# A third fixed expert whose gate-up is loaded as the routing begins, and routing tables moved out of its buffer

## The chip, the cores and the metric

The kernel runs on one core of a Trainium2 chip. The time is device microseconds of one execution, the median of three runs. The profile is of one more execution of the same program. TensorE (PE) multiplies and turns matrices, VectorE (DVE) and ScalarE (ACT) do element work, GpSimd (POOL) element work and indirect DMAs (gathers and scatters by row index), SP issues plain DMAs. All DMAs, whoever issues them, run on the core's 16 DMA engines.

## The reference, cut to what matters

The program is two layers of a decoder, 1024 tokens of 1024 channels, float32. Each layer is a mixer (attention with a state-space scan in layer 0, a convolution module in layer 1) and then a mixture of 32 experts, each token going to two. Only the mixture is touched:

```
g_sel = argmax(xt @ w_group + b_group)                 # 1 of 4 groups
top_v, top_i = top_k((xt @ w_expert)[group g_sel], 2)  # 2 of its 8 experts
gu = xb @ w_gate_up[e]                                 # 1024 x 1024 per expert
y  = (silu(gu[:, :512]) * gu[:, 512:]) @ w_down[e]     # 512 x 1024 per expert
out[token] += gate * y
```

An expert's weights are 4 MB (gate-up) and 2 MB (down); all 32 are read in each layer.

## The kernel before, in words

The function `moe(k, layer)` does one mixture. It has two stages.

Routing. TensorE turns the tokens and forms the logits, VectorE chooses groups and experts, ranks the tokens of each expert and builds index tables: `hidx` (which rows each expert gathers), `yidx` (where each result goes), `order` (the experts sorted by their token count) and the overflow lists. Meanwhile ScalarE writes the normalised rows `h` of all eight 128-token tiles, two at a time, into a staging buffer for four tiles and stores each pair to HBM (`h_rows`, 1 MB a store). The copy of tile 4 waits for the first store, that of tile 6 for the second (`h_stored`).

Experts. Three buffers for gate-up (`wgu[0..2]`, the first of them lies in `early_gu`) and three for down (`wd[0..2]`, the first in `early_wd`) are used in turn: place q of the sequence uses buffer q % 3. The first `FIXED` places hold experts 0, 1, ... in that order; the others are sorted by count and placed by `place_of`, so that places with more and with fewer tiles alternate. Each place has a fixed number of 32-token blocks (`CAP`), 84 blocks in all. For each place GpSimd gathers the rows (`gather`, three buffers), TensorE turns them (`turn_tokens`), and for each block does gate-up and, one block later, down; ScalarE and VectorE form the hidden rows, ScalarE copies the result out, GpSimd scatters it. SP issues the loads in a list in program order: the load of place q waits on `gu_done` (down: `d_done`) for place q-3.

Where the routing tables lie: in the third pair of buffers, `wgu[2]` (the staging rows `h` and a part of the tables) and `wd[2]` (the rest). So the loads into the third pair wait until the tables are done with: gate-up on `y_index`, down on `over_ready`. The lines on SP:

```
load_down(sp, 1, 1)
for n in range(2):
    sp.wait_ge(h_stored[n], 16 * NT // 4)
load_gate_up(sp, 1, 1)
sp.wait_ge(order_ready, 1)
for q in range(FIXED, NE):
    e = sp.value_load(order[0:1, q:q + 1], ...)
    if q == 2: sp.wait_ge(y_index, 1)
    else:      sp.wait_ge(gu_done, last_of[q - 3] + 1)
    load_gate_up(sp, e, q % 3)
    ...
```

The gate-up and down of expert 0 are loaded before the function begins. The first gathers wait for all stores (`h_stored`) and for `h_index`. "Gate-up 5" below means the gate-up load of place 5, counted from 0.

Of the kernel before, what the change touches and what calls it, by code (L numbers as in the profile page):

```python
# [21 lines left out]
P = 128  # L22
D = 1024
T = 1024
NT = T // P
KD = D // P
# [13 lines left out]
NG, EG = 4, 8  # L40
NE = NG * EG
FF = 512
KF = FF // P
# [3 lines left out]
LN_EPS = 1e-5  # L47
MAX_OVER = NE
TB = 32
FIXED, FULL, LARGE = 2, 2, 14  # L50


XB, YB = 3, 6
TURNS, LAST_FULL = 12, 18
SQUARED_EARLY = 6
LOGITS_EARLY = (0, 3)

# [906 lines left out]
def moe(k, layer):  # L964
# [13 lines left out]
    with ExitStack() as ctx:  # L978
# [2 lines left out]
        wgu12, wd12 = sb("wgu", [P, 2, KD, 2 * FF]), sb("wd", [P, 2, KF, D])  # L981
        wgu = [first_gate_up(k), wgu12[:, 0, :, :], wgu12[:, 1, :, :]]
        wd = [first_down(k), wd12[:, 0, :, :], wd12[:, 1, :, :]]
        third = [wgu[2].rearrange("p k n -> p (k n)"), wd[2].rearrange("p k n -> p (k n)")]
        behind = [k.early_gu[:, KD * 2 * FF + NE * n:KD * 2 * FF + NE * (n + 1)] for n in range(7)]
        used = [0, 0]

        def early(shape, b=0):
            n = math.prod(shape[1:])
            flat = third[b][:, used[b]:used[b] + n]  # L990
            used[b] += n
            assert used[b] <= (KD * 2 * FF, KF * D)[b]
            if len(shape) == 2:
                return flat
            names = "abc"[:len(shape) - 1]
            return flat.rearrange(f"p ({' '.join(names)}) -> p {' '.join(names)}", **dict(zip(names, shape[1:])))

        n_over = sb("n_over", [P, 1], I32)
        over_expert = sb("over_expert", [P, MAX_OVER], I32)
# [2 lines left out]
        yidx = sb("yidx", [P, P // TB, NE], I32)  # L1002

        ss, rstd = k.m_ss, k.m_rstd
        h = early([P, 4, D])
        xT = sb("xT", [P, 2, KD, P])
        L = k.logits
        strict = early([P, P], 1)
        desc = behind[0]
        eid = behind[1]  # L1010
        pos_row = early([P, P], 1)
        quarter = sb("quarter", [P, 1])
        iota_i = sb("iota_i", [P, P], I32)
        quarter_i = sb("quarter_i", [P, 1], I32)
# [1 line left out]
        slot_ids = sb("slot_ids", [P, 2, NT], I32)  # L1016
        slot_next = sb("slot_next", [P, 2 * NT])
        pad = sb("pad", [P, MAX_OVER], I32)
        scan_mask = early([P, NE, NT + 1])
        gm, gw, wm = sb("gm", [P, NT]), sb("gw", [P, NT]), sb("wm", [P, NT])  # L1020
        ge, go = sb("ge", [P, NT, NG]), sb("go", [P, NT, NG])
        E, W = early([P, NT, NE], 1), early([P, NT, NE], 1)
        M = early([P, 2, NT, NE], 1)
        M_flat = M[:, :, :, :].rearrange("p j i e -> p (j i) e")
        Msel = early([P, 2, NT, NE], 1)
        Msel_flat = Msel[:, :, :, :].rearrange("p j i e -> p (j i) e")
        both = early([P, NE, NT + 1], 1)
        top = [sb("top1_", [P, NT]), sb("top2_", [P, NT])]
        ex, den = sb("ex", [P, NT]), sb("m_den", [P, NT])
        pre = early([P, NE, NT + 1], 1)  # L1030
        rank = early([P, NE, NT], 1)
        rank_sel = early([P, 2 * NT])
        in_group, met = early([P, NT, EG]), early([P, NT, EG])
        key = early([P, NE], 1)
        cmp = early([P, NE, NE], 1)
        V_rank = cmp[:, 0:2 * NT, :]
        nth = early([P, NSORT], 1)
        up_to = early([P, NSORT], 1)
        place = early([P, NE], 1)
        V = early([P, 2 * NT, NE])  # L1040
        R = early([P, 2 * NT, P])
        tabT = early([P, P], 1)
        tabT_rows = early([P, P // TB, P])
        fold = behind[2]
        fold_sorted, place_col = early([P, NE]), early([P, 1])
        empty, wrap, hf = early([P, NE]), early([P, NE]), early([P, NE])
        empty_y, yf = early([P, P // TB, NE]), early([P, P // TB, NE])
        order_f = early([P, NE], 1)
        cap_e, excess = early([P, NE], 1), early([P, NE], 1)
        extra, incl, shift, oe = behind[3], behind[4], behind[5], sb("oe", [P, MAX_OVER])  # L1050
        one_row = behind[6]
        pos, posf = sb("pos", [P, 2 * NT], I32), sb("posf", [P, 2 * NT])

        xg = sb("xg", [P, XB, D])
        sg = sb("sg", [P, 2, P])
        hh = sb("hh", [P, 2, P])
        hhT = sb("hhT", [P, 2, P])
        y = sb("my", [P, YB, D // 4])
        over_y = R[:, 0:NT, :].rearrange("p n t -> p (n t)")
        over_hh = R[:, NT:NT + KF, :]  # L1060
        over_sg = R[:, NT + KF:2 * NT, :].rearrange("p n t -> p (n t)")
        over_slot = sb("over_slot", [P, 1], I32)
        over_h = sb("over_h", [P, 1])
        over_ih = sb("over_ih", [P, 1], I32)
# [10 lines left out]
        dve_link, pool_link = sem("m_dve_link"), sem("m_pool_link")  # L1075
        gu_loaded = [k.dma_sems[layer]["gu_loaded0"]] + [sem(f"gu_loaded{p}_") for p in range(1, 3)]
        wd_loaded = [k.dma_sems[layer]["wd_loaded0"]] + [sem(f"wd_loaded{p}_") for p in range(1, 3)]
        zeroed = sem("zeroed")
        gathered = [k.dma_sems[layer][f"gathered{n}"] for n in range(XB)]
        stored = [k.dma_sems[layer][f"stored{n}"] for n in range(YB)]  # L1080
        turned, xT_ready, gu_done, silu_ready, hh_ready = sem("e_turned"), sem("xT_ready"), sem("gu_done"), sem("silu_ready"), sem("hh_ready")
# [30 lines left out]
        @block.sync  # L1112
        def _(sp):
            sp.wait_ge(consts, 1)
            sp.dma_start(k.token_slot.rearrange("(p n) a -> p (n a)", p=P), pad[:]).then_inc(padded, 16)
            load_down(sp, 1, 1)
            for n in range(2):
                sp.wait_ge(h_stored[n], 16 * NT // 4)
            load_gate_up(sp, 1, 1)
            sp.wait_ge(order_ready, 1)  # L1120
            for q in range(FIXED, NE):
                e = sp.value_load(order[0:1, q:q + 1], min_val=0, max_val=NE - 1)
                if q == 2:
                    sp.wait_ge(y_index, 1)
                else:
                    sp.wait_ge(gu_done, last_of[q - 3] + 1)
                load_gate_up(sp, e, q % 3)
                if q == 2:
                    sp.wait_ge(over_ready, 1)
                else:  # L1130
                    sp.wait_ge(d_done, last_of[q - 3] + 1)
                load_down(sp, e, q % 3)
            if layer == 0:
                load_conformer_rows(k, sp)
                sp.wait_ge(d_done, last_of[NE - 2] + 1)
                for c in range(2):
                    load_conformer_w(k, sp, c, c)
            sp.wait_ge(gu_done, NB)
            sp.wait_ge(d_done, NB)
            for n in range(YB):  # L1140
                sp.wait_ge(stored[n], 16 * len(range(n, NB, YB)))
            sp.wait_ge(table_made, 16 * 2 * NT)
            sp.wait_ge(over_ready, 1)

            def over(j):
                sp.dma_start(over_slot[:], k.token_slot[bass.ds(j * P, P), :]).then_inc(o_idx, 16)
                e = sp.value_load(over_expert[0:1, at(j)], min_val=0, max_val=NE - 1)
                sp.dma_start(wgu[OVER], w_gu[at(e)].rearrange("a p k n -> p (a k) n")).then_inc(o_w, 16)
                sp.dma_start(wd[OVER], w_down[at(e)].rearrange("a p k n -> p (a k) n")).then_inc(o_w, 16)
                sp.wait_ge(o_stored, j * 16 + 16)  # L1150
                sp.sem_inc(sp_waited, 1)
            turns_over(sp, over)

            if layer == 1:
                for i in range(NT):
                    for j in range(2):
                        sp.dma_start(wgu[j][:, i, :], k.ybuf.rearrange("(j p n) d -> j p n d", j=2, n=NT)[j, :, i, :]).then_inc(y_loaded[i], 16)  # L1157
                for i in range(NT):
                    sp.wait_ge(x_sum, 2 * i + 2)
                    sp.dma_start(k.out[0, i * P:(i + 1) * P, :], x[:, i, :]).then_inc(out_done, 16)  # L1160
                sp.wait_ge(out_done, 16 * NT)

        @block.scalar
        def _(act):
# [5 lines left out]
            for i in range(NT):  # L1170
                if i == SQUARED_EARLY:
                    act.wait_ge(rstd_ready, 1)
                if i >= 4 and i % 2 == 0:
                    act.wait_ge(h_stored[i // 2 % 2], 16 * (i // 4))
                act.activation(h[:, i % 4, :].rearrange("q (k p) -> q k p", k=KD), x[:, i, :].rearrange("q (p k) -> q k p", k=KD),
                               ACT.Copy, scale=rstd[:, i:i + 1]).then_inc(h_ready, 1)
                if i % 2:
                    act.wait_ge(h_ready, i + 1)
                    act.dma_start(h_rows[:, i - 1:i + 1, :], h[:, i % 4 - 1:i % 4 + 1, :]).then_inc(h_stored[i // 2 % 2], 16)
# [30 lines left out]
        def _(pool):  # L1210
            link = Link(pool, pool_link)
            pool.memset(pad[:], PAD).then_inc(consts, 1)
            pool.memset(xg[:], 0.0).then_inc(zeroed, 1)
            late = slice(SQUARED_EARLY, NT)
            pool.wait_ge(squared, NT - SQUARED_EARLY)
            link(pool.tensor_scalar(ss[:, late], ss[:, late], 1.0 / D, RMS_EPS, ALU.mult, ALU.add))
# [46 lines left out]

            pool.wait_ge(chosen, 1)
            pool.tensor_tensor(V[:], M_flat, slot_next[:].unsqueeze(2).to_broadcast([P, 2 * NT, NE]), ALU.mult).then_inc(v_ready, 1)
            pool.wait_ge(zeroed, 1)
            for n in range(2):
                pool.wait_ge(h_stored[n], 16 * NT // 4)
            pool.wait_ge(h_index, 1)
            for q in range(FIXED):  # L1270
                gather(q)
            pool.wait_ge(h_index, 2)
            gather(2)
            pool.wait_ge(turned, 1)
            pool.wait_ge(gathered[0], 16)
            gather(XB)
# [899 lines left out]
```

## Time and profile before

| | |
|---|---|
| median of 3 runs | 2068.88 us (2068.82 to 2070.03) |
| span of the profiled execution | 2064.8 us |
| what lies around the span (median less span) | 4.1 us |
| busy: PE, DVE, POOL, ACT | 1872.5, 884.8, 439.8, 427.7 us |
| DMA | 525.19 MB, mean 254 GB/s |
| mixture of layer 0, of layer 1 (from the span's start) | about 500 to 1055, 1476 to the end |

The page gives the profiled execution's span; a time of its own beside the span is not listed, so the median of the runs stands for it. The span's 40 slices show the DMA engines at nine tenths or more through both expert stages and TensorE at eight to nine tenths there.

### The profile page before, as it was taken

How to read it: one execution, taken by the hardware profiler on the slowest of the kernel's cores; microseconds unless marked ns; L12 is line 12 of the kernel's file. 1: busy time of each engine (PE TensorE's matmuls, PEld its weight loads, DVE VectorE, ACT ScalarE, POOL GpSimd, SP SyncE). 2: the span in 40 equal slices, each digit the busy share in tenths (PEclk: the TensorE clock that was granted, in tenths of full speed). 3: DMA queues.
4: the chain of work that ended last, by engine and by line, in shares of the span. 5: the costliest groups of instructions: out<-in, count | busy, mean ns of one | idle time of the engine just before them, and what ended most of it. 6: DMA issues, size and time to landing. Idle time of an engine off the chain costs nothing. (4 is left out here: it accounts for less than half of the span.)

```text
span 2064.8 us, 47004 instructions
## 1 busy us (share of the span) xinstructions
PE 1872.5 (91%) x20566; PEld 1145.4 (55%) x20566; DVE 884.8 (43%) x1972; ACT 427.7 (21%) x965; POOL 439.8 (21%) x552
## 2 busy tenths in 40 slices
PE   7899999999699999889959999699879999898992
PEld 5677766666466655555645444355546665555551
DVE  3666675664721111111135999992361111111114
ACT  2433332335111111011123122223411111011010
POOL 2211111112122332222122111120222232221220
PEclk9999999999799999999979999899979999999996
DMA  9200000032799999999967456412289999999996
GB/s 322 78 11 1 11 10 10 0 123 82 280 399 418 426 423 423 424 425 427 417 249 210 89 109 133 106 31 82 103 354 402 413 425 427 425 424 425 422 378 256
DMA packets 92208, 525.19 MB, mean 254 GB/s; under 512 B 24134, under 2 KB 47738, under 8 KB 74600
## 3 DMA queue, kind: packets, MB, share of 16 engines
q1 hardware_dynamic: 66072, 462.35, 54.8%
q0 software_dynamic: 24064, 51.45, 9.0%
q10 hardware_dynamic: 1872, 8.44, 1.0%
q8 instruction: 160, 2.62, 0.5%
q14 instruction: 40, 0.33, 0.1%
HBM read 495.90 MB, written 34.66 MB: 257 GB/s over the span
## 5 line engine op out<-in xcount | busy, mean ns | idle before, releaser
L1368 PE MATMUL ps<-wgu,xT 128*32 128x256 f32 x7168 | 419.9, 387 | 31.6 <-issue 31.6
L1533 DVE TENSOR_TENSOR hh<-sg,ps 128x128 f32<-128x128 f32 x168 | 66.5, 396 | 704.0 <-ACT sg L1195 703.6
L1368 PEld LDWEIGHTS ps<-wgu,xT 128*32 128x32 f32 x7168 | 239.4, 112 | 188.8 <-issue 53.3
L1255 POOL DMA_INDIRECT y_rows<-my,yidx x168 | 166.6, 992 | 736.4 <-ACT my L1189 729.1
L1368 PE MATMUL ps<-early_gu,xT 128*32 128x256 f32 x3584 | 214.4, 393 | 16.4 <-issue 13.5
L1383 PE MATMUL ps<-wd,hhT 128*32 128x256 f32 x3584 | 213.8, 379 | 0.0
L1195 ACT ACTIVATE sg<-ps 128x128 f32<-128x128 f32 x168 | 46.5, 277 | 689.3 <-PE ps L1368 689.3
L1368 PEld LDWEIGHTS ps<-early_gu,xT 128*32 128x32 f32 x3584 | 118.4, 114 | 100.3 <-issue 29.4
L1383 PEld LDWEIGHTS ps<-wd,hhT 128*32 128x32 f32 x3584 | 119.3, 110 | 74.1
L2099 DVE SCALAR_TENSOR_TENSOR conv<-dd,par,conv 128x256 f32<-128x256 f32 (+1 forms) x255 | 131.4, 589 | 0.2
L800 PEld LDWEIGHTS ps<-m_hT,early_gu 128*128 128x128 f32 x1024 | 116.1, 192 | 4.6 <-issue 3.4
L800 PE MATMUL ps<-m_hT,early_gu 128*128 128x128 f32 x1024 | 116.9, 275 | 0.7 <-DMA early_gu<-in_w_in 0.7
L1189 ACT ACTIVATE my<-ps 128x256 f32<-128x256 f32 x168 | 64.4, 383 | 250.9 <-PE ps L1383 233.2
L1750 PE MATMUL ps<-c_hT,early_wd 128*128 128x512 f32 x256 | 112.7, 593 | 3.5 <-ACT sig L1911 3.3
L1786 PE MATMUL ps<-w_pw,c_hT 128*128 128x512 f32 x256 | 113.9, 599 | 1.5 <-ACT c_hT L1928 1.5
L1758 PE MATMUL ps<-c_hT,early_wd 128*128 128x512 f32 x256 | 112.5, 592 | 0.0
L1383 PE MATMUL ps<-early_wd,hhT 128*32 128x256 f32 x1792 | 107.2, 379 | 0.0
L1526 DVE TENSOR_TENSOR xT<-ps,g_exp 128x384 f32<-128x384 f32 (+2 forms) x128 | 58.9, 502 | 103.6 <-PE ps L1350 103.6
L854 PE MATMUL ps<-w_out_sb,m_yT 128*128 128x512 f32 x192 | 86.6, 604 | 0.0
L794 PE MATMUL ps<-w_in_sb,m_hT 128*128 128x264 f32 (+1 forms) x240 | 81.0, 491 | 4.7 <-DVE m_hT L623 4.7
L1750 PEld LDWEIGHTS ps<-c_hT,early_wd 128*128 128x128 f32 x256 | 48.4, 190 | 64.5 <-issue 64.1
L1758 PEld LDWEIGHTS ps<-c_hT,early_wd 128*128 128x128 f32 x256 | 48.6, 190 | 61.2 <-issue 61.2
(346 smaller groups left out, 2117.5 us busy)
## 6 DMA issues: line engine op xcount, KB each, us to landing
wgu<-in_moe_w_gate_up SPq DMA_DIRECT2D x42, 4096.0 KB, 31.8
early_gu<-in_moe_w_gate_up SPq DMA_DIRECT2D x22, 4096.0 KB, 31.5
wd<-in_moe_w_down SPq DMA_DIRECT2D x42, 2048.0 KB, 30.0
early_wd<-in_moe_w_down SPq DMA_DIRECT2D x22, 2048.0 KB, 30.1
early_wd<-in_conv_w_pw SPq DMA_DIRECT2D x22, 512.0 KB, 5.4
conv<-prod POOLq DMA_DIRECT2D x20, 512.0 KB, 4.5
h_rows<-wgu ACTq DMA_DIRECT2D x8, 1024.0 KB, 3.9
m_xT<-in_x_turned SPq DMA_DIRECT2D x8, 512.0 KB, 3.4
```

What stands on the lines that cost most here:

```text
L794: mm = pe.matmul(ps[:, bank, 0:n1 - n0], hT[:, j, :], w_z[:, j, :] if n0 == Z0 else w_in[:, j, n0:n1], start=(j == 0), stop=(j == KD - 1))
L800: mm = pe.matmul(ps[:, bank, (t % 4) * P:(t % 4 + 1) * P], w_x[:, j, t * P:(t + 1) * P], hT[:, j, :], start=(j == 0), stop=(j == KD - 1))
L854: mm = pe.matmul(ps[:, bank, :], attn_T[p][:, j, :] if j < 4 else yT[:, j, :], w_out[:, j, 512 * half:512 * half + 512], start=(j == 0), s ...
L1189: act.activation(y[:, n % YB, :], ps[:, Y + n % 2, 0:D // 4], ACT.Copy).then_inc(y_ready, 1)
L1255: pool.indirect_dma_start(out=y_quarters, out_offset=bass.IndirectOffsetOnAxis(ap=yidx[:, tl, q:q + 1], axis=0), in_=y[:, n % YB, :], in_o ...
L1368: mm = pe.matmul(ps[TB * g:TB * g + TB, GU + n % 2, 0:2 * P].rearrange("p (a f) -> p a f", a=2), xT[:, q % 2, j, TB * tl:TB * tl + TB], wg ...
L1383: mm = pe.matmul(ps[TB * g:TB * g + TB, Y + n % 2, 0:D // 4], hhT[:, n % 2, TB * j:TB * j + TB], wd[q % 3][:, j, D // 4 * g:D // 4 * g + D ...
L1533: tt(hh[:, n % 2, :].rearrange("q (k f) -> q k f", k=KF), by_k(sg[:, n % 2, :]), by_k(ps[:, GU + n % 2, P:2 * P]), ALU.mult).then_inc(hh_r ...
L1750: mm = pe.matmul(ps[:, GATE, :], wg[:, p, j, :], hT[:, j, HALF * h:HALF * h + HALF], start=(j == 0), stop=(j == KD - 1))
L1758: mm = pe.matmul(ps[:, LIN + n % 2, :], wa[:, p, j, :], hT[:, j, HALF * h:HALF * h + HALF], start=(j == 0), stop=(j == KD - 1))
L1786: mm = pe.matmul(ps[:, BACK + half, :], yT[:, j, :], w_pw2[:, j, 512 * half:512 * half + 512], start=(j == 0), stop=(j == CT - 1))
L2099: ins = dve.scalar_tensor_tensor(out=out[s], in0=dd[:, s, q + k0:q + k1], scalar=par[:, c, 2 * q - 1 + s:2 * q + s], in1=out[s] if r else ...
```

## The change

`FIXED` goes from 2 to 3, `LARGE` from 14 to 13 and `LAST_FULL` from 18 to 17: places 0 to 2 hold experts 0, 1 and 2 with three blocks each, the other 29 are sorted. The staging rows `h` move into the buffer of the gathered rows `xg` and result rows `y` (now one tensor, `rows_in_out`), the one-hot rows `R` into `xT`, `V` and others into the buffers of the hidden rows (`acts`), some small tables into `Msel`; the remaining tables stay in `wd[2]`. Nothing of the routing is left in `wgu[2]`, so SP loads expert 2's gate-up right at the start. The zeroing of `xg` is dropped.

```diff
-FIXED, FULL, LARGE = 2, 2, 14
+FIXED, FULL, LARGE = 3, 2, 13
-TURNS, LAST_FULL = 12, 18
+TURNS, LAST_FULL = 12, 17
...
-        h = early([P, 4, D])
+        rows_in_out = sb("rows_in_out", [P, XB * D + YB * (D // 4)])
+        xg = rows_in_out[:, 0:XB * D].rearrange("p (b n) -> p b n", b=XB)
+        y = rows_in_out[:, XB * D:].rearrange("p (b n) -> p b n", b=YB)
+        h = rows_in_out[:, 0:4 * D].rearrange("p (b n) -> p b n", b=4)
...
             load_down(sp, 1, 1)
+            load_gate_up(sp, 2, 2)
             for n in range(2):
                 sp.wait_ge(h_stored[n], 16 * NT // 4)
             load_gate_up(sp, 1, 1)
+            sp.wait_ge(over_ready, 1)
+            load_down(sp, 2, 2)
             sp.wait_ge(order_ready, 1)
             for q in range(FIXED, NE):
                 e = sp.value_load(order[0:1, q:q + 1], min_val=0, max_val=NE - 1)
-                if q == 2:
-                    sp.wait_ge(y_index, 1)
-                else:
-                    sp.wait_ge(gu_done, last_of[q - 3] + 1)
+                sp.wait_ge(gu_done, last_of[q - 3] + 1)
                 load_gate_up(sp, e, q % 3)
-                if q == 2:
-                    sp.wait_ge(over_ready, 1)
-                else:
-                    sp.wait_ge(d_done, last_of[q - 3] + 1)
+                sp.wait_ge(d_done, last_of[q - 3] + 1)
                 load_down(sp, e, q % 3)
...
+                if i == XB:
+                    act.wait_ge(squared, NT - SQUARED_EARLY)
...
-            pool.memset(xg[:], 0.0).then_inc(zeroed, 1)
...
-            for q in range(FIXED):
+            for q in range(XB):
                 gather(q)
             pool.wait_ge(h_index, 2)
-            gather(2)
```

On SP, at the start of the mixture of layer 0, the list before reads as follows. `wgu` and `wd` are the weight buffers; a wait stands on the instruction that it holds up.

```order
L1115 DMA token_slot<-pad 128x32 [waits m_consts0]
L1102 DMA wd<-in_moe_w_down 128x4096
L1099 DMA wgu<-in_moe_w_gate_up 128x8192 [waits h_stored1_0,h_stored0_0]
L1122 TENSOR_LOAD order [waits order_ready0]
L1122 ISA x2
L1099 ISA [waits y_index0]
L1099 DMA wgu<-in_moe_w_gate_up 128x8192
L1102 ISA [waits over_ready0]
L1102 DMA wd<-in_moe_w_down 128x4096
```

After the change the same place reads:

```order
L1122 DMA token_slot<-pad 128x32 [waits m_consts0]
L1109 DMA wd<-in_moe_w_down 128x4096
L1106 DMA wgu<-in_moe_w_gate_up 128x8192
L1106 DMA wgu<-in_moe_w_gate_up 128x8192 [waits h_stored1_0,h_stored0_0]
L1109 DMA wd<-in_moe_w_down 128x4096 [waits over_ready0]
L1132 TENSOR_LOAD order [waits order_ready0]
L1132 ISA x2
```

A gate-up load now stands without a wait between the first down load and the wait for the row stores; it is the one that stood behind `y_index`. The down load of the third pair keeps its wait.

On TensorE, in the expert loop of layer 0, the sequence before from the turning of place 3's rows (`xg`) on is this; x32 is one block's gate-up, x16 one block's down, and `early_gu` and `early_wd` are the first pair of buffers, which place 3 uses.

```order
L1350 MATMUL ps<-ident,xg 128x2x4x16 x8
L1368 MATMUL ps<-wgu,xT 32x256 x32
L1383 MATMUL ps<-wd,hhT 32x256 x16
L1368 MATMUL ps<-wgu,xT 32x256 x32
L1383 MATMUL ps<-wd,hhT 32x256 x16
L1368 MATMUL ps<-wgu,xT 32x256 x32
L1383 MATMUL ps<-wd,hhT 32x256 x16
L1368 MATMUL ps<-early_gu,xT 32x256 x32
L1383 MATMUL ps<-wd,hhT 32x256 x16
```

After the change, from the same turning on:

```order
L1353 MATMUL ps<-ident,rows_in_out 128x2x4x16 x8
L1371 MATMUL ps<-wgu,xT 32x256 x32
L1386 MATMUL ps<-wd,acts 32x256 x16
L1371 MATMUL ps<-wgu,xT 32x256 x32
L1386 MATMUL ps<-wd,acts 32x256 x16
L1371 MATMUL ps<-early_gu,xT 32x256 x32
L1386 MATMUL ps<-wd,acts 32x256 x16
```

Place 2 has one block fewer after the turning, and place 3 (`early_gu`) begins one block earlier; it has four blocks after the change and two before. The number of blocks in all is the same.

## Rows read from the trace of the kernel before

**Rows 1.** Stretch of layer 1's experts: engines' busy us, PEclk, DMA share, GB/s.

```profile
1640.00:1981.00 341.00, 319.01 (x5424) 194.95 (x5424) 58.25 (x152) 36.03 (x109) 90.43 (x90) 0.97 1.01 425
```

**Rows 2.** Timeline of SP's queue: start, us, line, DMA; layer 0, then layer 1.

```profile
524.16 0.33 SPq L1099 DMA_DIRECT2D wgu<-in_moe_w_gate_up  x1
...
1476.39 0.43 SPq L1102 DMA_DIRECT2D wd<-in_moe_w_down  x1
...
1500.13 0.33 SPq L1099 DMA_DIRECT2D wgu<-in_moe_w_gate_up  x1
...
1517.18 0.35 SPq L1099 DMA_DIRECT2D wgu<-in_moe_w_gate_up  x1
...
1533.27 0.33 SPq L1099 DMA_DIRECT2D early_gu<-in_moe_w_gate_up  x1
...
1583.37 0.33 SPq L1099 DMA_DIRECT2D early_gu<-in_moe_w_gate_up  x1
...
1981.74 0.33 SPq L1099 DMA_DIRECT2D wgu<-in_moe_w_gate_up  x1
```

**Rows 3.** Us to landing (last column) of gate-ups 5, 6 and 31, layer 1.

```profile
wgu<-in_moe_w_gate_up SPq DMA_DIRECT2D x1, 4096.0 KB, 13.9
...
early_gu<-in_moe_w_gate_up SPq DMA_DIRECT2D x1, 4096.0 KB, 18.4
...
wgu<-in_moe_w_gate_up SPq DMA_DIRECT2D x1, 4096.0 KB, 30.6
```

**Rows 4.** TensorE's timeline where the last place begins, layer 0 and layer 1.

```profile
1043.04 5.35 PE L1368 MATMUL ps<-wgu,xT 128*32 128x256 f32 x64 [3.40 <-issue]
...
2012.43 3.66 PE L1368 MATMUL ps<-wgu,xT 128*32 128x256 f32 x64 [0.95 <-issue]
```

**Rows 5.** Timeline: first turning, layer 0; first gather, turning, places 1 and 2, layer 1.

```profile
544.94 1.97 PE L1350 MATMUL ps<-ident,xg 128*128 128x128 f32 x8 [0.64 <-DMA xg<-h_rows,hidx]
...
1509.60 1.21 POOL L1248 DMA_INDIRECT xg<-h_rows,hidx  x1 [11.66 <-DVE hidx L1496]
...
1513.78 1.97 PE L1350 MATMUL ps<-ident,xg 128*128 128x128 f32 x8 [0.26 <-DMA xg<-h_rows,hidx]
...
1546.12 3.64 PE L1368 MATMUL ps<-wgu,xT 128*32 128x256 f32 x64
...
1551.30 3.64 PE L1368 MATMUL ps<-wgu,xT 128*32 128x256 f32 x64
```

**Rows 6.** Us to landing, layer 1: issued at 1476, 1482, 1487:1497, 1500, 1517.

```profile
wd<-in_moe_w_down SPq DMA_DIRECT2D x1, 2048.0 KB, 7.8
...
h_rows<-wgu ACTq DMA_DIRECT2D x1, 1024.0 KB, 4.7
...
h_rows<-wgu ACTq DMA_DIRECT2D x3, 1024.0 KB, 3.8
...
wgu<-in_moe_w_gate_up SPq DMA_DIRECT2D x1, 4096.0 KB, 12.3
...
wgu<-in_moe_w_gate_up SPq DMA_DIRECT2D x1, 4096.0 KB, 14.0
xg<-h_rows,hidx POOLq DMA_INDIRECT x1, 13.5
```

**Rows 7.** GpSimd's timeline in the routing of layer 1.

```profile
1496.89 1.05 POOL L1265 TENSOR_TENSOR wgu<-wd,slot_next 128x512 f32<-128x512 f32 x1 [10.25 <-DVEq L1464]
```

**Rows 8.** Us to landing, layer 0: first gather (at 540), fourth (at 547).

```profile
xg<-h_rows,hidx POOLq DMA_INDIRECT x1, 4.5
...
xg<-h_rows,hidx POOLq DMA_INDIRECT x1, 9.7
```

**Rows 9.** ScalarE's timeline, layer 1: first store, fifth copy, last store.

```profile
1482.34 0.33 ACTq L1179 DMA_DIRECT2D h_rows<-wgu  x1
...
1487.38 4.19 ACT L1175 ACTIVATE wgu<-x_res,m_rstd 128x1024 f32<-128x1024 f32 x2 [0.40 <-DMA h_rows<-wgu]
...
1496.22 0.33 ACTq L1179 DMA_DIRECT2D h_rows<-wgu  x1
```

More of the change, by code:

```diff
@@ L983, in moe, with shaped @@
         wd = [first_down(k), wd12[:, 0, :, :], wd12[:, 1, :, :]]
-        third = [wgu[2].rearrange("p k n -> p (k n)"), wd[2].rearrange("p k n -> p (k n)")]
+        tables = wd[2].rearrange("p k n -> p (k n)")
         behind = [k.early_gu[:, KD * 2 * FF + NE * n:KD * 2 * FF + NE * (n + 1)] for n in range(7)]
[L986 to L992, printed above, removed]
+        used = [0]
+        def shaped(flat, shape):
             if len(shape) == 2:
@@ L996, in early, with part_of @@
             return flat.rearrange(f"p ({' '.join(names)}) -> p {' '.join(names)}", **dict(zip(names, shape[1:])))
+        def early(shape):
+            n = math.prod(shape[1:])
+            flat = tables[:, used[0]:used[0] + n]
+            used[0] += n
+            assert used[0] <= KF * D, used
+            return shaped(flat, shape)
+        def part_of(flat, at0, shape):
+            return shaped(flat[:, at0:at0 + math.prod(shape[1:])], shape)
         n_over = sb("n_over", [P, 1], I32)
@@ L1004, in moe @@
         ss, rstd = k.m_ss, k.m_rstd
-        h = early([P, 4, D])
         xT = sb("xT", [P, 2, KD, P])
+        acts = sb("acts", [P, 6 * P])
+        rows_in_out = sb("rows_in_out", [P, XB * D + YB * (D // 4)])
+        xg = rows_in_out[:, 0:XB * D].rearrange("p (b n) -> p b n", b=XB)
+        y = rows_in_out[:, XB * D:].rearrange("p (b n) -> p b n", b=YB)
+        h = rows_in_out[:, 0:4 * D].rearrange("p (b n) -> p b n", b=4)
+        y_spare = rows_in_out[:, 4 * D:]
         L = k.logits
-        strict = early([P, P], 1)
+        strict = early([P, P])
         desc = behind[0]
         eid = behind[1]
-        pos_row = early([P, P], 1)
+        pos_row = early([P, P])
         quarter = sb("quarter", [P, 1])
@@ L1018, in moe @@
         pad = sb("pad", [P, MAX_OVER], I32)
-        scan_mask = early([P, NE, NT + 1])
         gm, gw, wm = sb("gm", [P, NT]), sb("gw", [P, NT]), sb("wm", [P, NT])
         ge, go = sb("ge", [P, NT, NG]), sb("go", [P, NT, NG])
-        E, W = early([P, NT, NE], 1), early([P, NT, NE], 1)
-        M = early([P, 2, NT, NE], 1)
+        E, W = early([P, NT, NE]), early([P, NT, NE])
+        M = early([P, 2, NT, NE])
         M_flat = M[:, :, :, :].rearrange("p j i e -> p (j i) e")
-        Msel = early([P, 2, NT, NE], 1)
+        Msel = early([P, 2, NT, NE])
@@ L1026, in moe @@
+        in_Msel = Msel[:, :, :, :].rearrange("p j i e -> p (j i e)")
+        scan_mask = part_of(in_Msel, 0, [P, NE, NT + 1])
+        in_group, met = part_of(in_Msel, 288, [P, NT, EG]), part_of(in_Msel, 352, [P, NT, EG])
+        rank_sel, fold_sorted = part_of(in_Msel, 416, [P, 2 * NT]), part_of(in_Msel, 432, [P, NE])
+        empty, place_col = part_of(in_Msel, 464, [P, NE]), part_of(in_Msel, 496, [P, 1])
         Msel_flat = Msel[:, :, :, :].rearrange("p j i e -> p (j i) e")
-        both = early([P, NE, NT + 1], 1)
+        both = early([P, NE, NT + 1])
@@ L1028, in moe @@
         top = [sb("top1_", [P, NT]), sb("top2_", [P, NT])]
         ex, den = sb("ex", [P, NT]), sb("m_den", [P, NT])
[L1030 to L1035, printed above, removed]
-        V_rank = cmp[:, 0:2 * NT, :]
-        nth = early([P, NSORT], 1)
-        up_to = early([P, NSORT], 1)
-        place = early([P, NE], 1)
@@ L1040, in moe @@
[L1040 to L1043, printed above, removed]
-        fold = behind[2]
[L1045 to L1049, printed above, removed]
+        pre = early([P, NE, NT + 1])
@@ new lines, in moe @@
+        rank = early([P, NE, NT])
+        key = early([P, NE])
+        cmp = early([P, NE, NE])
+        V_rank = cmp[:, 0:2 * NT, :]
+        nth = early([P, NSORT])
+        up_to = early([P, NSORT])
+        place = early([P, NE])
+        V = part_of(acts, 0, [P, 2 * NT, NE])
+        R = xT[:, :, :, :].rearrange("p b k t -> p (b k) t")
+        tabT = early([P, P])
+        tabT_rows = part_of(y_spare, 0, [P, P // TB, P])
+        fold = behind[2]
+        wrap, hf = early([P, NE]), early([P, NE])
@@ L1050, in moe @@
+        empty_y, yf = part_of(acts, 512, [P, P // TB, NE]), part_of(acts, 640, [P, P // TB, NE])
+        order_f = early([P, NE])
+        cap_e, excess = early([P, NE]), early([P, NE])
         extra, incl, shift, oe = behind[3], behind[4], behind[5], sb("oe", [P, MAX_OVER])
@@ L1052, in moe @@
         pos, posf = sb("pos", [P, 2 * NT], I32), sb("posf", [P, 2 * NT])
[L1054 to L1061, printed above, removed]
+        sg, hh, hhT = (part_of(acts, 2 * P * n, [P, 2, P]) for n in range(3))
+        over_room = wd[(OVER + 1) % 3]
+        over_y, over_sg = over_room[:, 0, :], over_room[:, 1, 0:FF]
+        over_hh = over_room[:, 2, 0:FF].rearrange("p (k t) -> p k t", k=KF)
         over_slot = sb("over_slot", [P, 1], I32)
@@ L1077, in moe @@
         wd_loaded = [k.dma_sems[layer]["wd_loaded0"]] + [sem(f"wd_loaded{p}_") for p in range(1, 3)]
-        zeroed = sem("zeroed")
         gathered = [k.dma_sems[layer][f"gathered{n}"] for n in range(XB)]
@@ L1265, in _ @@
             pool.tensor_tensor(V[:], M_flat, slot_next[:].unsqueeze(2).to_broadcast([P, 2 * NT, NE]), ALU.mult).then_inc(v_ready, 1)
-            pool.wait_ge(zeroed, 1)
             for n in range(2):
```

## The prediction

> **What bounds the kernel now.** I read the table by stretches first, then TensorE's timeline at the end of each layer, then SP's queue and the landings of the DMAs it issues. In the 341 us stretch of the second layer's experts that [rows 1] shows, the 16 DMA engines are busy throughout (share 1.01, 425 GB/s), while TensorE works 319 of the 341 us. So 22 us of it are waits, and the weight loads set the pace. The end confirms it: the last gate-up load is issued at 1981.74 [rows 2] and lands 30.6 us later [rows 3], at 2012.34, and TensorE starts the last expert at 2012.43 after a wait [rows 4]. In layer 0 it waits 3.40 us for the same load [rows 4]. Each layer therefore ends a fixed stretch of transfers after the moment from which the queue never runs dry. Whatever moves that moment moves the end by as much; a load taken out ahead of it gains nothing.
>
> The early stages set that moment. The load of expert 3 waits until TensorE has finished expert 0 (the wait on `gu_done` in the SP loop), and TensorE starts expert 0 when the first gather of rows has landed: in layer 1 TensorE's turning of these rows starts at 1513.78, in layer 0 at 544.94, and in both the gather ends the wait [rows 5]. That makes the first gather of each layer the place to look.
>
> **What the change takes away.** The third gate-up (index 2) was issued at 1517.18 [rows 2] and took 14.0 us [rows 6], landed 1531.2. TensorE first needs it at 1551.30 [rows 5]: 20 us to spare. The next load, expert 3's at 1533.27 [rows 2], comes after it has landed and waits for TensorE, not for the queue. So moving it to 1476.8 (right behind the down load at 1476.39) shortens nothing that anything waits for: **0**. The memset of the row buffers and its semaphore go too: it stands at the head of GpSimd's list, and GpSimd idles 10.25 us at the end of that part of it [rows 7], which hides it: **0**. Without that cover it would be worth its own length, at most some 6 us a layer (ScalarE writes 8 KB a partition in 4.19 us [rows 9], the memset writes 12 KB). The new wait of the scalar engine for its own squares is met by then: 0. The tables keep their shapes and their engines, and `over_ready` still comes from the same step of VectorE.
>
> **What it adds: company for the row stores.** ScalarE writes the normalised rows, two tiles at a time, into a staging buffer that holds four, and stores each pair. The fifth copy waits for the first store, the seventh for the second; the second-slot gate-up (index 1) and the first gathers wait for all of them. Today a store runs alone: 3.8 us; the first one meets the tail of the down load and takes 4.7 [rows 6]. After the change 4 MB of gate-up sit in the queue from 1476.8 on and start moving when the down load is through (issued 1476.39, 7.8 us to landing [rows 2, 6]; its data end near 1483). No row of before shows a store beside a gate-up. The nearest is a gather beside one: the fourth gather of each layer is issued about 1 us before gate-up 2 and takes 13.5 us in layer 1 [rows 6] and 9.7 in layer 0, where one alone takes 4.5 [rows 8]. It ends near the end of the gate-up, so the two take turns piece by piece and the small transfer is stretched to the length of the large one. A gate-up is 128 rows of 32 KB, 8 for each of the 16 engines; at 425 GB/s [rows 1] that is 9.9 us. A store is 128 rows of 8 KB, also 8 per engine, 2.5 us. Turn for turn both end after 12.4 us (my estimate from these rows), so a store costs between 3.8 us (untouched) and some 13; I take the far end, because the gathers' rows lie there.
>
> Layer 1, step by step, with the times of [rows 9]:
> - The first store is issued at 1482.34, as now, but ends at 1483 + 12.4 + 0.5 = 1495.9 instead of 1482.34 + 4.7 = 1487.0.
> - The fifth copy, now at 1487.38, starts at 1495.9: 8.5 late. The second store sits behind the first and is through by 1498.5, in time for the seventh copy. The last store is issued at 1496.22 + 8.5 = 1504.7 and lands 3.8 later, at 1508.5.
> - Gate-up 1, issued at 1500.13 today [rows 2] when the last store is in, goes out at 1508.6 and has the engines until about 1520 (12.3 us alone [rows 6]).
> - The first gather is issued at 1509.60, when its indices are ready [rows 5]; the stores are in just then, so its issue hardly moves. Today gate-up 1 is through as it begins. After the change it runs beside some 7 of gate-up 1's 8 rows per engine: its data begin near 1511.5 (issue 1.21 us long, and a little), 7 x 1.24 for the gate-up's rows and 8 x 0.15 for its own 4 KB rows at 425 GB/s give 1521.4, landing near 1521.7 instead of 1513.7. **+8.0 us**, with bounds 0 (stores untouched) and +9.0 (13.5 - 4.5, the most that a gather beside a gate-up has cost). The later gathers and the whole expert loop queue behind it. TensorE has nothing else to do there.
>
> Layer 0: here the routing takes longer after the stores. Gate-up 1 goes out at 524.16 now [rows 2]; 8.5 later is 532.7, and it has the engines until about 544. TensorE takes the first gather's rows at 544.94 [rows 5], 4.5 us after its issue [rows 8], so that is near 540.4; it begins to move near 542, so it shares the engines with the last one or two rows of gate-up 1 per engine: **+2.0 us**, bounds 0 and +5.2 (9.7 - 4.5).
>
> **The order of sizes.** The sequence of tile counts goes from 3,3,4,2,4,2,3 to 3,3,3,4,2,4,2; the blocks stay 84. Load k waits for expert k-3, so gate-up 5 is issued one block (1551.30 - 1546.12 = 5.18 us [rows 5]) earlier and gate-up 6 one block later. Gate-up 5 finds an empty queue now (13.9 us to landing, near the 12.3 alone) and gate-up 6 a full one (18.4) [rows 3]; afterwards it is the other way round. In layer 1: 6 lands now at 1583.37 + 18.4 = 1601.8 [rows 2]; after, 1588.55 + 13.9 = 1602.4. That is **+0.6**, and I take the same for layer 0. Bounds -4.0 a layer (13.9 less 9.9 of data: the one gap filled and no other opened) and +5.2 (the whole block lost). The last two-tile expert of the mixed part now stands at index 26, so TensorE waits for gate-up 27 instead, which lies inside the stretch that the loads bound: 0.
>
> **Sum.** 8.0 + 2.0 + 0.6 + 0.6 = +11.2 us. The profiled execution spans 2064.8 us; the median of the runs is 2068.88, so 4.1 us lie around the span. 2064.8 + 11.2 + 4.1 gives **2080.1 us**, 0.54% slower. A difference under 0.2% (4.1 us) I call the same.
>
> **The rivals.**
> - *Whole transfers take turns.* An engine might finish one transfer's share before it takes up the other queue's. The first store would then slip in ahead of gate-up 2, the second would wait 9.9 us for it: 1487.0 + 9.9 + 2.5 + 0.5 = 1499.9; two copies (4.2) and the last store (3.8) make 1507.9, and the first gather would wait for all of gate-up 1: +7.3 in layer 1 and, since gate-up 1 of layer 0 would be through at 542, 0 there. With the 1.2 of the order: +8.5, 2077.4. Against it: the 9.7 us of layer 0's fourth gather [rows 8] are neither the 4.5 of one that goes ahead of a gate-up nor the 14 and more of one behind all of it. The Trainium skill, DMA: Bandwidth & Descriptors, section Queues, rings and completion order, says that an engine goes round the queues packet by packet, some 9 to 17 descriptors at a time; by it the sum would be this rival's. I trust the row more.
> - *The stores keep their pace*, sharing by bytes and not by turns. They would land some 4 us late, and gate-up 1 would overlap the first gather of layer 1 a little: between +1.2 (order alone) and +5, that is 2070.1 to 2074. For it: no row shows a store beside a gate-up. Against: the first store already pays 0.9 us for the tail of a down load.
> - *Faster: a load less in the bound stretch.* If the queue were already never empty at 1517, taking 4 MB out of it would end each layer 9.9 us earlier: -19.8 + 1.2, 2050.3. It decides itself at gate-up 3, which would have to be issued earlier than 1533.27 [rows 2] though its issue waits for TensorE. Against it: the 20 us to spare above. A milder form, only the empty stretch ahead of gate-up 5 filled, gives -8.0 for both layers, 2060.9.
> - *Worse*: the gather of layer 0 pays its far bound too (+3.2 more), or the order does (+4.6 a layer): 2083 to 2089.
> - *An overflow of the new fixed expert* (96 places) would add a pass of several loads after the loop. With these inputs the reference routes 74 and 85 tokens to it: excluded.
>
> The Trainium skill, same page, section Issuing engines are not separate DMA queues, speaks against the change in general: DMAs of different issuers interleave on the same 16 engines, so an early load is not free for the stores. The stretched gathers agree with it.
>
> **How the numbers follow.** Forecast (turn by turn, both layers, 2076 to 2084): 0.52. Whole transfers: 0.14. Stores keep their pace: 0.15, half of it within 0.2%. Worse: 0.07. Faster in either form: 0.12. So faster 0.12, same 0.09, slower 0.79. The range 2071 to 2088 holds all but the faster case, the lower end of the unhurt stores and the far end of the worse one.
>
> **What would show it.** In the profile after: ScalarE idle some 8 us ahead of the fifth copy, ended by a store; SP's gate-up 1 of layer 1 some 32 us after that down load, now 23.7; TensorE's first turning in layer 1 some 45.4 us after the layer's down load is issued on SP, now 37.4; the same in layer 0 about 2 us later than now; gate-up 6 with some 14 us to landing and gate-up 5 with more; the bound stretch as long as before. If the fifth copy does not wait, the store step is wrong and the time stays near 2070; if gate-up 3 starts earlier against the layer's start, the faster rival is right.

## The result and the profile after

| | before | after |
|---|---|---|
| median, 6 runs each | 2069.29 us (2064.98 to 2070.06) | 2079.51 us (2075.72 to 2084.93) |
| span of the profiled execution | 2064.8 us | 2075.7 us |

The ratio is 1.0052, 95% interval [1.0036, 1.0067]: the change makes the kernel about 10 us slower. The profiled execution of after took 2077.54 us, so 1.8 us lie around its span. The reading follows the chain from the first row stores on.

ScalarE's timeline of after, layer 1 (start, us, line, operation, idle before it and what ended it): first store, fifth copy, last store.

```profile
1484.46 0.33 ACTq L1185 DMA_DIRECT2D h_rows<-rows_in_out  x1
...
1499.38 4.19 ACT L1181 ACTIVATE rows_in_out<-x_res,m_rstd 128x1024 f32<-128x1024 f32 x2 [10.30 <-DMA h_rows<-rows_in_out]
...
1508.31 0.33 ACTq L1185 DMA_DIRECT2D h_rows<-rows_in_out  x1
```

The fifth copy, which waited 0.40 us before [rows 9], now waits 10.30 us, and a row store ends the wait. The DMA issues of after, layer 1, with the us to landing in the last column, give the store's own time: the first store, the second, and the last two.

```profile
h_rows<-rows_in_out ACTq DMA_DIRECT2D x1, 1024.0 KB, 14.9
...
h_rows<-rows_in_out ACTq DMA_DIRECT2D x1, 1024.0 KB, 12.7
...
h_rows<-rows_in_out ACTq DMA_DIRECT2D x2, 1024.0 KB, 3.8
```

4.7 us for the first store [rows 6] became 14.9, and the two stores that meet no gate-up still take 3.8. The DMA queues of after from 1488 to 1496 (packets, MB, share of 16 engines' time; q1 is SP's queue, q10 ScalarE's) show how the two share:

```profile
q1 hardware_dynamic: 85, 2.79, 83.8%
q10 hardware_dynamic: 85, 0.70, 20.8%
```

There are 85 packets on each side, and a packet here is one row: 32 KB of the gate-up, 8 KB of the store. In the records of single rows, every one of the 72 store rows that start between 1487.8 and 1495 is followed at once by a row of the gate-up, so the two take turns by single rows. The store gets a fifth of the bytes, because its rows are a quarter as long.

SP's queue of after, layer 1: down load, gate-up 1, gate-up 3, gate-up 5, gate-up 6 and the last gate-up.

```profile
1478.51 0.42 SPq L1109 DMA_DIRECT2D wd<-in_moe_w_down  x1
...
1512.17 0.33 SPq L1106 DMA_DIRECT2D wgu<-in_moe_w_gate_up  x1
...
1545.62 0.35 SPq L1106 DMA_DIRECT2D early_gu<-in_moe_w_gate_up  x1
...
1578.81 0.33 SPq L1106 DMA_DIRECT2D wgu<-in_moe_w_gate_up  x1
...
1600.91 0.33 SPq L1106 DMA_DIRECT2D early_gu<-in_moe_w_gate_up  x1
...
1990.89 0.33 SPq L1106 DMA_DIRECT2D wgu<-in_moe_w_gate_up  x1
```

Gate-up 1 goes out 33.66 us after the down load; before it was 23.74 [rows 2]. In the timeline of GpSimd and TensorE after, this is what the first gather of layer 1 and the first turnings of layers 0 and 1 make of it:

```profile
547.55 1.97 PE L1353 MATMUL ps<-ident,rows_in_out 128*128 128x128 f32 x8 [3.00 <-DMA rows_in_out<-h_rows,hidx]
...
1512.96 1.50 POOL L1253 DMA_INDIRECT rows_in_out<-h_rows,hidx  x1 [12.54 <-DMA h_rows<-rows_in_out]
...
1525.34 1.97 PE L1353 MATMUL ps<-ident,rows_in_out 128*128 128x128 f32 x8 [10.63 <-DMA rows_in_out<-h_rows,hidx]
```

The gather is now released by a store, no longer by its indices [rows 5], and the turning starts 12.38 us after the gather's issue instead of 4.18. Between the two lies gate-up 1, issued 0.8 us ahead of the gather. The queues from 1513 to 1518 and from 1518 to 1524 (q0 is GpSimd's):

```profile
q1 hardware_dynamic: 64, 2.10, 111.0%
...
q1 hardware_dynamic: 64, 2.10, 80.9%
q0 software_dynamic: 64, 0.26, 10.6%
```

In the first five microseconds the gather moves nothing, and then it alternates with gate-up 1, 64 rows to 64; each of these 64 rows of the gather is again followed at once by one of the gate-up. All 128 rows of gate-up 1 lie in these 11 us; half of the gather's 128 rows are still to come. The stretch that the loads bound is as it was in [rows 1] (after; busy us of PE, PEld, DVE, ACT, POOL, then PEclk, DMA share and GB/s):

```profile
1652.00:1992.00 340.00, 321.53 (x5470) 204.19 (x5464) 59.45 (x155) 36.34 (x110) 90.48 (x90) 0.98 1.01 425
```

Gate-up 3 and the last gate-up are issued 445.3 us apart, 448.5 before [rows 2]. So the time was lost ahead of this stretch. The 10.9 us of span come together like this, each stretch against before: 2.8 from layer 0's down load to its first turning, 9.4 in the same stretch of layer 1, and -1.3 in all that remains (start -0.2, loop of layer 0 +2.4, from its last gate-up issue to layer 1's down load -2.9, loop of layer 1 -2.4, end +1.8).

### The profile page after: what moved, and what is told of

Its sections match the earlier page's. It is cut to its first block and busy times, and to the rows that moved or that the text cites. A ratio compares the mean times of both kernels' runs of the same rounds, so it can differ in the third digit from the quotient of the medians.

```text
span 2075.7 us, 46986 instructions
## 1 busy us (share of the span) xinstructions
PE 1877.4 (90%) x20566; PEld 1163.0 (56%) x20566; DVE 885.2 (43%) x1972; ACT 427.3 (21%) x965; POOL 434.4 (21%) x550
## 5 line engine op out<-in xcount | busy, mean ns | idle before, releaser
L1536 DVE TENSOR_TENSOR acts<-acts,ps 128x128 f32<-128x128 f32 x168 | 67.0, 399 | 703.5 <-ACT acts L1201 703.2
L1260 POOL DMA_INDIRECT y_rows<-rows_in_out,yidx x168 | 166.6, 992 | 733.2 <-ACT rows_in_out L1195 723.3
L1371 PE MATMUL ps<-early_gu,xT 128*32 128x256 f32 x3712 | 223.0, 391 | 15.1 <-issue 12.9
L1386 PE MATMUL ps<-wd,acts 128*32 128x256 f32 x3520 | 217.5, 379 | 0.0
L1201 ACT ACTIVATE acts<-ps 128x128 f32<-128x128 f32 x168 | 46.6, 277 | 694.4 <-PE ps L1371 694.4
L1386 PEld LDWEIGHTS ps<-wd,acts 128*32 128x32 f32 x3520 | 124.8, 110 | 70.9 <-issue 0.3
L1386 PE MATMUL ps<-early_wd,acts 128*32 128x256 f32 x1856 | 117.2, 379 | 0.0
L1195 ACT ACTIVATE rows_in_out<-ps 128x256 f32<-128x256 f32 x168 | 64.4, 384 | 246.1 <-PE ps L1386 235.5
L1386 PEld LDWEIGHTS ps<-early_wd,acts 128*32 128x32 f32 x1856 | 67.6, 110 | 36.8 <-issue 0.8
L1753 PEld LDWEIGHTS ps<-c_hT,early_wd 128*128 128x128 f32 x256 | 49.0, 192 | 65.7 <-issue 65.3
```

The lines of the kernel that those rows point to most:

```text
L1195: act.activation(y[:, n % YB, :], ps[:, Y + n % 2, 0:D // 4], ACT.Copy).then_inc(y_ready, 1)
L1260: pool.indirect_dma_start(out=y_quarters, out_offset=bass.IndirectOffsetOnAxis(ap=yidx[:, tl, q:q + 1], axis=0), in_=y[:, n % YB, :], in_o ...
L1371: mm = pe.matmul(ps[TB * g:TB * g + TB, GU + n % 2, 0:2 * P].rearrange("p (a f) -> p a f", a=2), xT[:, q % 2, j, TB * tl:TB * tl + TB], wg ...
L1386: mm = pe.matmul(ps[TB * g:TB * g + TB, Y + n % 2, 0:D // 4], hhT[:, n % 2, TB * j:TB * j + TB], wd[q % 3][:, j, D // 4 * g:D // 4 * g + D ...
L1536: tt(hh[:, n % 2, :].rearrange("q (k f) -> q k f", k=KF), by_k(sg[:, n % 2, :]), by_k(ps[:, GU + n % 2, P:2 * P]), ALU.mult).then_inc(hh_r ...
L1753: mm = pe.matmul(ps[:, GATE, :], wg[:, p, j, :], hT[:, j, HALF * h:HALF * h + HALF], start=(j == 0), stop=(j == KD - 1))
```

## The experiments

The first three form a square with the change itself: are the stores stretched, and does a gate-up lie beside the first gather? They and the fourth ran together, with a median of 2068.34 us for the kernel before.

**Neither: gate-up 2 back in its old place.** The rest of the change stays.

```diff
             load_down(sp, 1, 1)
-            load_gate_up(sp, 2, 2)
...
             load_gate_up(sp, 1, 1)
+            sp.wait_ge(y_index, 1)
+            load_gate_up(sp, 2, 2)
             sp.wait_ge(over_ready, 1)
```

> The change with one load put back: gate-up 2 stands behind gate-up 1 and the wait on the result table, as before; the moved tables, the third fixed expert and the order of sizes stay. Theory (the early gate-up 2 stretches the row stores to some 15 us, so that gate-up 1 and with it the first gather come late): the stores take 3.8 to 4.7 us again, gate-up 1 of layer 1 is issued 23.7 us after the down load (33.7 with the change), the first turning 37.4 us after it, and the time is that of before, 2066 to 2072 us. Rival (the new layout or the new order of sizes costs the time): it stays at 2076 us or more although the stores are short.

Measured: 2066.93 us, ratio 0.9993 [0.9979, 1.0007]. ScalarE's and TensorE's timeline of this kernel, layer 1:

```profile
1489.05 4.20 ACT L1182 ACTIVATE rows_in_out<-x_res,m_rstd 128x1024 f32<-128x1024 f32 x2 [0.40 <-DMA h_rows<-rows_in_out]
...
1515.41 1.97 PE L1354 MATMUL ps<-ident,rows_in_out 128*128 128x128 f32 x8 [1.18 <-DMA rows_in_out<-h_rows,hidx]
```

The fifth copy waits 0.40 us again and the turning starts 37.35 us after the down load (1478.06). The whole loss hangs on this one load's place; moved tables, dropped memset, third fixed expert and order together cost nothing that these runs can tell.

**Stretched stores, but no gate-up beside the gather.** Gate-up 2 stays early, gate-up 1 is held back.

```diff
             for n in range(2):
                 sp.wait_ge(h_stored[n], 16 * NT // 4)
+            sp.wait_ge(y_index, 1)
             load_gate_up(sp, 1, 1)
```

> The change with gate-up 2 still loaded at the start, but gate-up 1 held back until the result table is made, so that no gate-up lies beside the first gather. Theory (late stores cost only through gate-up 1 beside the first gather): the stores still take some 15 us, but the first gather takes about 4.5 us instead of 13 and is issued only some 1.2 us late in layer 1, so about 2070.5 us (2068 to 2073). Rival (the late stores cost by themselves, whatever lies beside the gather): 2077 us or more.

Measured: 2070.91 us, 1.0013 [1.0000, 1.0026]. ScalarE, GpSimd and TensorE in the timeline of this kernel, layer 1:

```profile
1497.55 4.20 ACT L1182 ACTIVATE rows_in_out<-x_res,m_rstd 128x1024 f32<-128x1024 f32 x2 [11.37 <-DMA h_rows<-rows_in_out]
...
1511.14 1.28 POOL L1254 DMA_INDIRECT rows_in_out<-h_rows,hidx  x1 [13.99 <-DMA h_rows<-rows_in_out]
...
1515.40 1.97 PE L1354 MATMUL ps<-ident,rows_in_out 128*128 128x128 f32 x8 [2.74 <-DMA rows_in_out<-h_rows,hidx]
```

The fifth copy waits even longer than in the change, yet the turning follows the gather's issue by 4.26 us. What remains is that the gather itself is issued late: 35.54 us after the down load (1475.60), 33.21 before. That is 2.3 us late instead of the 1.2 expected, though the time is within the expected range. Late stores by themselves cost these 2.3 us; the medians stand 2.6 apart.

**Stores on time, but gate-ups beside the gather.**

```diff
             load_down(sp, 1, 1)
-            load_gate_up(sp, 2, 2)
...
             load_gate_up(sp, 1, 1)
+            load_gate_up(sp, 2, 2)
```

> The change with gate-up 2 issued right behind gate-up 1, both when the last row store is in; nothing lies beside the stores, but a gate-up lies beside the first gather of layer 1. Theory (the price is paid at the first gather): the stores take 3.8 us as before, the first gather of layer 1 lands some 8 us late and that of layer 0 some 2 to 5, so 2078 to 2084 us. Rival (the stretched stores are what costs): 2067 to 2071 us.

Measured: 2078.86 us, 1.0050 [1.0036, 1.0063], the loss of the change. ScalarE's and TensorE's timeline of this kernel, layer 1:

```profile
1490.73 4.20 ACT L1181 ACTIVATE rows_in_out<-x_res,m_rstd 128x1024 f32<-128x1024 f32 x2 [0.40 <-DMA h_rows<-rows_in_out]
...
1526.26 1.97 PE L1353 MATMUL ps<-ident,rows_in_out 128*128 128x128 f32 x8 [9.44 <-DMA rows_in_out<-h_rows,hidx]
```

No copy waits, and still the turning starts 46.51 us after the down load (1479.75), where the change has 46.83. The price is paid at the gather, whichever way a gate-up gets beside it; the stretched stores were the way by which this change brought it there.

**The early gate-up 2 in shorter rows.** Same bytes, four loads of 8 KB rows.

```diff
-            load_gate_up(sp, 2, 2)
+            for j in range(4):
+                part = slice(2 * j, 2 * j + 2)
+                sp.dma_start(wgu[2][:, part, :], w_gu[at(2)].rearrange("a p k n -> p (a k) n")[:, part, :]).then_inc(gu_loaded[2], 16)
...
```

Left out: TensorE's wait on the load counts all four parts.

> The change with the early gate-up 2 cut into four loads of 128 rows of 8 KB each instead of one of 128 rows of 32 KB; bytes, buffer and place in the list are the same. Theory (the queues take turns row by row, so a store of 8 KB rows loses as many bytes to its neighbour as the neighbour's rows hold): beside 8 KB rows the first store takes some 6 to 8 us instead of 15, ends near the down load's end plus 5 us, gate-up 1 goes out at most 2 us later than before, and the time is 2068 to 2073 us. Rival (a store beside a gate-up is stretched to the end of the whole 4 MB, however it is cut): the stores take some 15 us again and the time is 2077 us or more.

Measured: 2072.00 us, 1.0020 [1.0010, 1.0029]. The time is the theory's; the store is between the two. DMA queues of this kernel from 1487 to 1495, then ScalarE's fifth copy and TensorE's first turning in its timeline:

```profile
q10 hardware_dynamic: 225, 1.71, 50.9%
q1 hardware_dynamic: 230, 1.67, 49.7%
```

```profile
1493.76 4.16 ACT L1183 ACTIVATE rows_in_out<-x_res,m_rstd 128x1024 f32<-128x1024 f32 x2 [6.28 <-DMA h_rows<-rows_in_out]
...
1519.80 1.97 PE L1355 MATMUL ps<-ident,rows_in_out 128*128 128x128 f32 x8 [6.71 <-DMA rows_in_out<-h_rows,hidx]
```

These are 225 packets to 230, of which 16 and 26 are of 4 bytes: 209 rows to 204, now half of the bytes each. Row for row holds, and cutting the neighbour's rows helps. But the first store took 10.9 us, not 6 to 8, since it was issued at 1482.86 and moved nothing until 1486.5 (158 packets on q1 in that time, none on q10). So gate-up 1, whose rows are still 32 KB long, went out 6.2 us late against the down load, not 2, and met the first gather of layer 1: the turning follows the gather's issue (1509.18) by 10.6 us. In layer 0 it did not meet the gather, and the turning came 4.3 us after its issue (540.86, 545.15), no later than before.

**Both gate-ups after the stores, in shorter rows**, as in the third run but each cut into four. This run and the next three were taken together, beside a kernel before with a median of 2069.20 us.

```diff
-            load_gate_up(sp, 1, 1)
-            load_gate_up(sp, 2, 2)
+            for p in range(1, 3):
+                for j in range(4):
+                    part = slice(2 * j, 2 * j + 2)
+                    sp.dma_start(wgu[p][:, part, :], w_gu[at(p)].rearrange("a p k n -> p (a k) n")[:, part, :]).then_inc(gu_loaded[p], 16)
...
```

Left out: TensorE's waits on the two loads count all four parts.

> Gate-ups 1 and 2 both issued when the last row store is in, gate-up 1 first, as in the run that came to 2078.9 us, but each cut into four loads of 128 rows of 8 KB. Theory (the queues take turns row by row, also beside a gather): the first gather of layer 1, of 4 KB rows, takes 6 to 7.5 us beside 8 KB rows instead of some 13 beside 32 KB rows, and the time falls by half or more of the 10 us lost there: 2070 to 2074 us. Rival (the gather waits for all that is ahead in the other queue): 2078 us or more.

Measured: 2074.55 us, 1.0034 [1.0021, 1.0047], a little above the expected range. TensorE's timeline of this kernel, layer 1, and its DMA queues from 1514.5 to 1518.3 and from 1518.5 to 1521:

```profile
1523.15 1.97 PE L1355 MATMUL ps<-ident,rows_in_out 128*128 128x128 f32 x8 [4.75 <-DMA rows_in_out<-h_rows,hidx]
```

```profile
q1 hardware_dynamic: 213, 1.61, 100.4%
...
q1 hardware_dynamic: 109, 0.76, 72.2%
q0 software_dynamic: 91, 0.28, 27.5%
```

The turning follows the gather's issue (1514.47) by 8.7 us, against 13.4 with the long rows: again the cut helps, and again some 4 us pass before the gather moves its first row. That wait does not get shorter with the neighbour's rows. The 2.4 us by which it exceeds the 1.9 of a gather alone are about what the gather took beyond the 6 to 7.5 us expected. In layer 0, where the gate-ups are almost through when the gather starts, the cut gave nothing (7.7 us against 7.3).

**The order of sizes alone.** The kernel before with the three constants; gate-up 2 keeps its place and its wait.

```diff
-FIXED, FULL, LARGE = 2, 2, 14
-TURNS, LAST_FULL = 12, 18
+FIXED, FULL, LARGE = 3, 2, 13
+TURNS, LAST_FULL = 12, 17
...
```

Left out: place 2 is now a fixed one, so its two loads stand ahead of SP's loop, behind the same waits, and its gather moves into GpSimd's loop over the fixed places.

> The kernel before with the three constants of the change alone (three fixed experts, so the order of sizes 3,3,3,4,2,4,2 at the start); the tables lie in the third gate-up buffer and gate-up 2 is loaded where it was. Theory (the order of sizes is worth next to nothing: gate-up 5 comes a block earlier and finds a full queue, gate-up 6 a block later and finds an empty one): 2067 to 2071 us, my forecast of the term being +1.2. Rival (the order costs a whole block a layer, +10): 2077 us or more. Rival (it fills the gap ahead of gate-up 5 and opens no other, -8): 2061 us or less.

Measured: 2068.53 us, 1.0009 [0.9999, 1.0018]: between nothing and +3.7 us (the two medians stand 0.7 us apart the other way, so the sign is not shown). The forecast of +1.2 lies in it, and both rivals are out. The DMA's busy tenths in 40 equal slices from 1533 to 1640, each 2.7 us, show why the order gives nothing: the kernel before, then this run.

```profile
DMA  9999979999989785998999998999899999999999
```

```profile
DMA  8999989999999999998962999999999999999989
```

The soft place is in the 14th to 16th slice before, around the issue of gate-up 5 at 1571.85, and in the 21st and 22nd in this run, ahead of gate-up 6 at 1590.88. One dry stretch was traded for another.

**A try at filling both.** The kernel before with the smaller place first in each pair (2 blocks, then 4), and the same on top of the second run.

```diff
-    return min(2 * nth, nth + TURNS) if nth < LAST_FULL else 2 * (nth - LAST_FULL) + 1
+    return min(2 * nth + 1, nth + TURNS) if nth < LAST_FULL else 2 * (nth - LAST_FULL)
...
```

Left out: the same formula on VectorE, which places the sorted experts.

> The kernel before with the order of sizes turned round: places with fewer tiles come first in each pair (2 blocks, then 4) instead of places with more. Theory (the queue runs dry ahead of gate-up 5 and 7, whose loads wait for a long place; the loads bound the stretch behind): both gaps of some 5 us a layer are filled and the kernel gains 8 to 11 us: 2057 to 2061 us. Rival (the gaps only move to other places, as with the order of the change): 2066 us or more.

Measured: 2063.58 us, 0.9978 [0.9966, 0.9990], faster than both kernels, by about half of what was expected. Its DMA slices from 1531 to 1640:

```profile
DMA  9999999999999999999999999999999999989999
```

The soft place is gone. Over 1535 to 1640 the DMA engines are busy 1.00 of the time and move 420 GB/s; before it was 0.98 and 409. That is 1.2 MB more, 2.7 us at 425 GB/s, per layer if both are alike: 5.4 us, near the 5.6 between the medians. It is a rough account: in this execution the way from the first turning to the last gate-up's issue is 2.4 us shorter in layer 1 and 1.4 us in layer 0. I had taken the whole slack ahead of gate-ups 5 and 7 as gain; the slices of before stand at five to eight tenths ahead of gate-up 5, so a good half of that was in use.

> The change with gate-up 1 held back until the result table is made and with the places with fewer tiles first in each pair. Theory (both early costs gone and the gaps filled): some 8 to 11 us below the same without the turned order (2070.9), 2060 to 2063 us. Rival (the order is worth nothing): 2070 us or more.

Measured: 2066.75 us, 0.9989 [0.9975, 1.0003]. That is 4.2 us below the second run (each beside its own kernel before, whose medians lie 0.9 apart), about half of what was expected again.

## Why the prediction was right

Forecast +11.2 us of span, 2080.1 us; measured 10.9 us in the profiled execution and 2079.51 us. The mechanism held link by link, but the sizes did not: the two gathers cost 2.2 us more than forecast (9.4 and 2.8 for 8.0 and 2.0) and all the rest 2.5 us less (-1.3 for +1.2), so that the sum agrees to 0.3 us is in part luck.

- **Taking gate-up 2 from its place, the memset, the moved tables: 0.** Right as a sum: without the early load all of it together stands at 0.9993. The memset was not tried by itself; in the trace of before it takes 2.66 us in each layer, well under the 6 that I allowed it.
- **The store is stretched to the gate-up's length.** Right, and too short: 14.9 us in layer 1 against 13.6 (1495.9 less 1482.34). The fifth copy came 9.9 us late against the down load, not 8.5, and so did the last store and gate-up 1. I had the store take its turns from the gate-up's first row on. It begins 3.4 us after its issue (below), and from 1487 to 1497, in which the gate-up moves its last 98 rows, the store has moved 90 of its 128; the other 38 follow alone.
- **The first gather of layer 1: +8.0.** Measured +9.4. The step that failed is "its issue hardly moves": the last store comes 9.9 us late, so the gather waits for it and is issued 1.2 us late. The gather beside gate-up 1 then gave +8.2, within 0.2 of the forecast, but for another reason: I had it move from 1.9 us after its issue, turn for turn, with 7 rows of gate-up 1 per engine; it moved after 5.7 us, found some 4 rows left, and was held to the end of the gate-up with half of its rows. The later start and the fewer rows happen to cancel. My bound of +9.0 was also misread: 13.5 us is not the most that a gather beside a gate-up took before, for the one issued at 1532.20, beside gate-up 3, took 17.8 us to land.
- **Layer 0: +2.0.** Measured +2.8: the turning follows the gather's issue by 6.9 us instead of 4.5, with gate-up 1 out 10.4 us late instead of 8.5, and the gather itself is issued 0.4 us later. The 0.4 is not the load's doing: in the first run, with the stores on time, the gather of layer 0 is as late.
- **The order: +0.6 a layer.** Measured between -0.1 and +1.9 a layer with the constants alone; what is left of the change's own span is -1.3, of which -0.2 is its start. Half of the trade that I described is there. The landings of the loads are not in the trace of after, but the records of the single rows are: gate-up 6 finds an empty queue, as forecast (first row 1.0 us after its issue, last one through after 13.2; before 5.0 and 17.9). Gate-up 5 does not find the full one that I gave it (2.0 and 14.0 us; before 1.0 and 13.2); it is gate-up 7 that now waits behind others (5.2 and 18.1; before 1.0 and 13.6). Counted from the first turning, gate-up 6 is through 1.3 us later than before and gate-up 7 0.2 us earlier, so little is left of the trade by then.
- **Whole transfers take turns: refuted.** The first store would have slipped in ahead of gate-up 2; it took 14.9 us, with 85 rows to 85. The Trainium skill, DMA: Bandwidth & Descriptors, section Queues, rings and completion order, has an engine drain a packet of some 9 to 17 descriptors before it switches. A store is 8 rows on each engine; if a row is one descriptor, by that it would have got through in one turn. Here the measurement decides: the turns are single rows.
- **The stores keep their pace: refuted** by the same rows. **Faster: refuted**; gate-up 3 waits for TensorE as before (20.3 us after the first turning, 19.5 before), so a load less ahead of it gained nothing. The milder form, a filled gap ahead of gate-up 5, is true of that gap alone: the next one opened. **Worse** did not come about.
- **Two readings of the sum.** Not all of the 4.1 us lie around the span: the six runs of after have 1.7 to 1.9 us there, so the profiled execution of before was probably some 2.3 us faster than the median. The forecast adds 11.2 to the median either way and stands. And that TensorE's waits in [rows 4] are for the last load follows from the times, since the rows themselves name no releaser: in layer 0 the load is issued at 1009.90 and lands 33.0 us later, 0.1 us before TensorE starts.

## What to carry to other kernels

A load moved early is only free if nothing that others wait for shares the DMA engines with it. Here the queues took turns row by row, so a transfer with short rows was stretched to nearly the length of one with as many long rows: look for small stores and gathers between the load's new start and its end, follow who waits for them, and price the last one in the chain. What was lost here was not at the stretched stores but two steps on, at the one gather that TensorE waits for; and cutting the long rows into four buys back part of it.

## What the runs showed that I had not expected

A transfer that meets busy DMA engines starts late as well as moving slowly. The times are those of the first rows in the records of each queue. Alone, the third store of layer 1 after the change moves its first row 0.8 us after its issue; the first, beside a gate-up, after 3.4 us (3.9 beside rows of 8 KB). For a gather it is 1.9 us alone (layer 1 before), 5.7 beside a gate-up (layer 1 after) and 4.3 in the third run, and 4.3 to 4.5 when the gate-ups are cut into 8 KB rows. So the wait does not scale with the neighbour's rows. What sets it no run here shows, and it stays open.
